# RWKV scan of a hybrid decoder: some 64x64 products moved to the other head's partitions, and the first transposed inverse made by TensorE

## What is computed

```
def step(S, inp):
    r_t, w_t, k_t, v_t, kk_t, a_t = inp
    sa = jnp.einsum('bhvk,bhk->bhv', S, -kk_t)
    S = (S * w_t[:, :, None, :] + sa[..., None] * (kk_t * a_t)[:, :, None, :]
         + v_t[..., None] * k_t[:, :, None, :])
    return S, jnp.einsum('bhvk,bhk->bhv', S, r_t)
...
S, y = lax.scan(step, S0.astype(jnp.float32), (tm(rh), tm(decay), tm(kh), tm(vh), tm(kk), tm(ah)))
```

## Time and profile before

| | us |
|---|---|
| median of three runs | 3128.39 (3128.33 to 3129.97) |
| the profiled execution | 3125.38 |
| its span, first to last instruction | 3123.7 |
| the scan's first score product and last state product | 920.6 and 1189.0 |
| from one step to the next | 16.4 |

### The profile page before, as it was taken

One profiled execution on the slowest core, in us unless ns is written; L12 is line 12 of the kernel. 1 busy time (PEld: TensorE's weight loads), 2 busy tenths in 40 slices (PEclk: granted clock), 3 DMA queues, 4 the chain that ended last, 5 costly groups with the idle time before them and its releaser, 6 DMA issues.

```text
span 3123.7 us, 75122 instructions
## 1 busy us (share of the span) xinstructions
PE 2958.1 (95%) x30609; PEld 2794.0 (89%) x30609; DVE 1578.3 (51%) x2270; ACT 1048.9 (34%) x2014; POOL 1336.7 (43%) x954
## 2 busy tenths in 40 slices
PE   6998999988989998899999899989999899899998
PEld 6997999978878886799998699879999799799998
DVE  3436666037258876576612251466660344476612
ACT  3224333225443333433322443343332322433322
POOL 3443544442335554254544263434444344254543
PEclk8999999999999999999999899999999899899999
DMA  7552333543420002333355232433336343133332
GB/s 260 166 166 86 89 95 100 189 117 113 145 49 4 4 4 65 108 96 95 88 181 150 69 123 78 139 116 92 92 100 202 111 151 108 55 96 94 90 88 88
DMA packets 465625, 332.69 MB, mean 107 GB/s; under 512 B 19914, under 2 KB 435608, under 8 KB 465122
## 3 DMA queue, kind: packets, MB, share of 16 engines
q1 hardware_dynamic: 461400, 325.24, 33.9%
q10 hardware_dynamic: 4010, 4.22, 0.6%
HBM read 319.62 MB, written 10.20 MB: 106 GB/s over the span
## 4 chain that ended last, share of the span: by engine, by line
PE 61%; DVE 5%; ACT 2%; issue 1%; POOL 0%; DVEq 0%; ACTq 0%
PE bank L1578 32%; PE bank L1586 16%; PE bank L2026 6%; PE bank L1601 1%; DVE h L2497 1%; PE bank L1539 1%; PE bank L1876 1%; PE bank L1607 1%; DVE proj L2442 0%; DVE mmt L2775 0%; PE bank L1668 0%; DVE rstd L2388 0%; DVE bd_B L2744 0%; PE bank L2167 0%; DVE bd_K L2739 0%
## 5 line engine op out<-in xcount | busy, mean ns | idle before, releaser
L741 POOL TENSOR_TENSOR w_lo<-w_raw,w_hi 128x1024 fp32r<-128x1024 f32 x404 | 1023.3, 2534 | 1199.4 <-ACT w_hi L937 1178.9
L1578 PE MATMUL bank<-u_hi,w_hi 128*128 128x260 f32 x4064 | 831.5, 286 | 15.7 <-ACT w_hi L937 9.4
L1578 PE MATMUL bank<-u_lo,w_hi 128*128 128x260 f32 x4064 | 821.9, 283 | 0.0
L1578 PEld LDWEIGHTS bank<-u_hi,w_hi 128*128 128x128 f32 x4064 | 623.4, 188 | 31.1 <-issue 19.3
L1578 PEld LDWEIGHTS bank<-u_lo,w_hi 128*128 128x128 f32 x4064 | 626.2, 188 | 1.8
L937 ACT ACTIVATE w_hi<-w_raw 128x1024 fp32r<-128x1024 f32 x402 | 424.4, 1056 | 477.6 <-PE bank L1586 240.7
L1586 PE MATMUL bank<-u_hi,w_lo 128*128 128x260 f32 x4064 | 528.1, 282 | 0.0
L1586 PEld LDWEIGHTS bank<-u_hi,w_lo 128*128 128x128 f32 x4064 | 502.4, 187 | 1.7
L1578 PE MATMUL bank<-hid_hi,w_hi 128*128 128x260 f32 x1664 | 337.6, 284 | 0.0
L1578 PE MATMUL bank<-hid_lo,w_hi 128*128 128x260 f32 x1664 | 335.0, 283 | 0.0
L2927 DVE TENSOR_TENSOR csb<-proj 128x520 f32 (+1 forms) x42 | 29.7, 707 | 486.6 <-ACT proj L1002 486.6
(11 more groups left out here) (461 smaller groups left out, 4062.9 us busy)
## 6 DMA issues: line engine op xcount, KB each, us to landing
w_raw<-in_ffn_w_up_dram SPq DMA_DIRECT2D x176, 512.0 KB, 3.6
...
```

What stands on the lines that cost most here:

```text
L741: pool.tensor_tensor(w_lo[:, s, :, :], w_raw[:, s, :, :], w_hi[:, s, :, :].bitcast(F32), ALU.subtract).then_inc(lo_done, 1)
L1578: pe.matmul(tile_ps[slot][half][0:width, 0:HALF], w_hi[:, s, k, 0:width], x[:, k0 + k, half * HALF:(half + 1) * HALF], start=start and k = ...
```

## The change

All of it is in the scan. A product that reads one head's partitions and writes the other's is called crossed.

- t1, the right side and the new transpose are crossed; so t1 and `rhs_sb` lie on the other head's partitions. t1 goes to columns 128 to 255 of bank 2g instead of 0 to 127.
- The transposed inverse is kept on the other head's partitions too.
- The first update product (to the inverse) reads the other head's partitions and writes its own: crossed, into bank 2g. The second (to the transpose) reads and writes the other head's: straight, into bank 2g+1. VectorE's addition reads both banks, which are now one tensor `banks`, with a four-dimensional pattern. u is crossed and comes back to its own partitions.
- GpSimd makes only the first inverse, with one multiplication by `low_mask` and one addition over all four tiles. TensorE transposes it behind the keys (`turn_inverse`, four tiles, crossed, into the upper half of bank 0). ScalarE copies it to `mmt` ahead of the y copy (`turned_inverse`). The counts of `tok_done` and `tok_ready` go up by one a step.
- New waits: TensorE's t1 and VectorE's addition at level 0 wait for that copy; TensorE waits for `inv_ready` already at the transpose, with y and the state update behind it.
- `inv_mask` and the ScalarE copies that filled it, once at the start, go.

The diff, without the declaration and the filling of `inv_mask`:

```diff
@@ -250,3 +249,4 @@
 
-        bank = [ctx.enter_context(nc.psum_tensor(f"bank{i}", [P, 512], F32)) for i in range(8)]
+        banks = ctx.enter_context(nc.psum_tensor("banks", [P, 8 * 512], F32))
+        bank = [banks[:, i * 512:(i + 1) * 512] for i in range(8)]
         tile_ps = [(bank[0], bank[1]), (bank[2], bank[3])]
@@ -849,11 +849,7 @@
                         idb = head_ident[:, :].unsqueeze(1).to_broadcast([P, 4, HD])
-                        both = inv_mask[:, :, :].rearrange("p two t -> p (two t)").unsqueeze(1).to_broadcast([P, 2, P])
-                        for g in range(2):
-                            gs = slice(2 * g, 2 * g + 2)
-                            pool.tensor_tensor(mmt[q][:, gs, :], sc[q][:, gs, 0:2 * HD], both, ALU.mult)\
-                                .then_inc(inv_masked, 1)
-                        for g in range(2):
-                            pool.wait_ge(inv_masked, 2 * w + g + 1)
-                            mv = mmt[q][:, 2 * g:2 * g + 2, :].rearrange("p i (two t) -> p (i two) t", two=2)
-                            pool.tensor_tensor(mv, mv, idb, ALU.add).then_inc(inv_ready, 1)
+                        pairs = low_mask[:, :].unsqueeze(1).to_broadcast([P, 4, HD])
+                        inv = mmt[q][:, :, 0:HD]
+                        pool.tensor_tensor(inv, sc[q][:, :, 0:HD], pairs, ALU.mult).then_inc(inv_masked, 1)
+                        pool.wait_ge(inv_masked, w + 1)
+                        pool.tensor_tensor(inv, inv, idb, ALU.add).then_inc(inv_ready, 1)
 
@@ -1347,3 +1341,3 @@
                         for i, (n, bk) in enumerate(((2, 4), (0, 1), (1, 3))):
-                            act.wait_ge(tok_done, 3 * w + i + 1)
+                            act.wait_ge(tok_done, 4 * w + i + 1)
                             act.activation(tok[:, :, n * HD:(n + 1) * HD],
@@ -1351,2 +1345,8 @@
 
+                    def turned_inverse(w, q):
+
+                        act.wait_ge(tok_done, 4 * w + 4)
+                        act.activation(mmt[q][:, :, HD:2 * HD], bank[0][:, 4 * HD:8 * HD].rearrange("p (i t) -> p i t", i=4),
+                                       ACT.Copy).then_inc(tok_ready, 1)
+
                     def scan_step(c, q, one_more, two_more):
@@ -1358,3 +1358,3 @@
                                 act.activation(t1[:, 2 * g:2 * g + 2, :],
-                                               bank[2 * g][:, 0:2 * HD].rearrange("p (i t) -> p i t", i=2),
+                                               bank[2 * g][:, 2 * HD:4 * HD].rearrange("p (i t) -> p i t", i=2),
                                                ACT.Copy).then_inc(t1_ready, 1)
@@ -1375,2 +1375,4 @@
                            .then_inc(uu_ready, 1)
+                        if one_more:
+                            turned_inverse(w + 1, 1 - q)
                         act.wait_ge(y_mm, w + 1)
@@ -1383,2 +1385,3 @@
 
+                    turned_inverse(0, 0)
                     tokens_out(0)
@@ -2022,2 +2025,6 @@
 
+                    def far(rs):
+
+                        return heads[1 - rs.start // HD]
+
                     def both(out, left, right, start=True, stop=True):
@@ -2054,2 +2061,10 @@
 
+                    def turn_inverse(w, q):
+
+                        pe.wait_ge(inv_ready, w + 1)
+                        for i in range(4):
+                            mm = both(lambda rs: bank[0][far(rs), (4 + i) * HD:(5 + i) * HD], lambda rs: mmt[q][rs, i, 0:HD],
+                                      lambda rs: ident[rs, rs])
+                        mm.then_inc(tok_done, 1)
+
                     def turn_values(c, q):
@@ -2070,7 +2085,8 @@
                                 else:
-                                    pe.wait_ge(inv_ready, 2 * w + g + 1)
+                                    pe.wait_ge(inv_ready, w + 1)
+                                    pe.wait_ge(tok_ready, 4 * w + 1)
                                 for i in range(2):
                                     z = 2 * g + i
-                                    mm = both(lambda rs: bank[2 * g][rs, i * HD:(i + 1) * HD], lambda rs: ct[rs, z, :],
-                                              lambda rs: mmt[q][rs, z, 0:HD])
+                                    mm = both(lambda rs: bank[2 * g][far(rs), (2 + i) * HD:(3 + i) * HD],
+                                              lambda rs: ct[rs, z, :], lambda rs: mmt[q][rs, z, 0:HD])
                                 mm.then_inc(t1_mm, 1)
@@ -2079,5 +2095,5 @@
                                 pe.wait_ge(st_updated, w + 1)
-                                pe.wait_ge(tok_ready, 3 * w + 1)
+                                pe.wait_ge(tok_ready, 4 * w + 2)
                                 for i in range(4):
-                                    o = lambda rs: bank[4][rs, i * HD:(i + 1) * HD]
+                                    o = lambda rs: bank[4][far(rs), i * HD:(i + 1) * HD]
                                     both(o, lambda rs: b["ZR"][rs, i, 0:HD], lambda rs: rw_ST[rs, 4 * q + i, :], True, False)
@@ -2086,3 +2102,3 @@
                                 mm.then_inc(rhs_mm, 1)
-                                pe.wait_ge(tok_ready, 3 * w + 3)
+                                pe.wait_ge(tok_ready, 4 * w + 4)
                             if one_more and lvl < 4:
@@ -2099,9 +2115,8 @@
                                 for i in range(2):
-                                    z = 2 * g + i
-                                    o = bank[2 * g + 1]
+                                    z, cs = 2 * g + i, slice(i * HD, (i + 1) * HD)
                                     if lvl < len(LEVELS) - 1:
-                                        both(lambda rs: o[rs, 2 * i * HD:(2 * i + 1) * HD], lambda rs: mmt[q][rs, z, HD:2 * HD],
-                                             lambda rs: t1[rs, z, :])
-                                    mm = both(lambda rs: o[rs, (2 * i + 1) * HD:(2 * i + 2) * HD], lambda rs: t1[rs, z, :],
-                                              lambda rs: mmt[q][rs, z, HD:2 * HD])
+                                        both(lambda rs: bank[2 * g][rs, cs], lambda rs: mmt[q][far(rs), z, HD:2 * HD],
+                                             lambda rs: t1[far(rs), z, :])
+                                    mm = both(lambda rs: bank[2 * g + 1][far(rs), cs], lambda rs: t1[far(rs), z, :],
+                                              lambda rs: mmt[q][far(rs), z, HD:2 * HD])
                                 mm.then_inc(d_mm, 1)
@@ -2116,4 +2131,4 @@
                                 pe.wait_ge(mmt_ready, 10 * w + 9 + i // 2)
-                            mm = both(lambda rs: bank[5][rs, i * HD:(i + 1) * HD], lambda rs: mmt[q][rs, i, HD:2 * HD],
-                                      lambda rs: rhs_sb[rs, i, :])
+                            mm = both(lambda rs: bank[5][rs, i * HD:(i + 1) * HD], lambda rs: mmt[q][far(rs), i, HD:2 * HD],
+                                      lambda rs: rhs_sb[far(rs), i, :])
                         mm.then_inc(u_mm, 1)
@@ -2122,2 +2137,3 @@
                             turn_keys(qn)
+                            turn_inverse(w + 1, qn)
                         pe.wait_ge(uu_ready, w + 1)
@@ -2144,2 +2160,3 @@
                     turn_keys(0)
+                    turn_inverse(0, 0)
                     pe.wait_ge(sample_columns_ready, 1)
@@ -2771,7 +2788,11 @@
                                 else:
-                                    dve.wait_ge(inv_ready, 2 * w + g + 1)
-                                dv = bank[2 * g + 1][:, 0:4 * HD].rearrange("p (i t) -> p i t", i=2)
-                                lo = 0 if lvl < len(LEVELS) - 1 else HD
-                                dve.tensor_tensor(mmt[q][:, gs, lo:2 * HD], mmt[q][:, gs, lo:2 * HD], dv[:, :, lo:2 * HD],
-                                                  ALU.add).then_inc(mmt_ready, 1)
+                                    dve.wait_ge(tok_ready, 4 * w + 1)
+                                if lvl < len(LEVELS) - 1:
+                                    dv = banks[:, 1024 * g:1024 * g + 1024].rearrange("p (b c) -> p b c", b=2)[:, :, 0:2 * HD]
+                                    dv = dv.rearrange("p b (i t) -> p i b t", i=2)
+                                    inv = mmt[q][:, gs, :].rearrange("p i (b t) -> p i b t", b=2)
+                                else:
+                                    dv = bank[2 * g + 1][:, 0:2 * HD].rearrange("p (i t) -> p i t", i=2)
+                                    inv = mmt[q][:, gs, HD:2 * HD]
+                                dve.tensor_tensor(inv, inv, dv, ALU.add).then_inc(mmt_ready, 1)
                             if one_more and lvl < 4:
@@ -2780,3 +2801,3 @@
                                 dve.wait_ge(exp_done, w + 3)
-                                dve.wait_ge(tok_done, 3 * w + 3)
+                                dve.wait_ge(tok_done, 4 * w + 3)
                                 build(c + 1, q)
```

3 lines of the change are left out of this document (removed).

## The result

The changed kernel takes 3107.61 us, the median of five runs from 3104.74 to 3112.66, against 3128.39 for the kernel before in the same comparison (five runs, 3123.04 to 3129.97): a ratio of 0.9935, with a 95% interval of 0.9923 to 0.9947. Predicted were 3108 and a range of 3102 to 3122. The number fits. What it was added up from does not: one term was far too small, another was missing, and the two nearly cancel. That the number came out is luck.

What follows compares the result with a forecast made beforehand. TensorE was taken to bound levels 0 and 1 and the tail, VectorE levels 2 and 3. Fourteen full steps at 1.20 (16.8), step 14 1.8, step 15 0.9, start 0.9: 3128.4 - 20.4 = 3108 us; range 3102 to 3122.

Steps and rivals of the forecast that it cites:

- Updates in four quarters, 8 slots to 4: Scan levels: a pair's update records take 4 slots (one record of each head together), gaining 0.23 us where TensorE bounds.
- Level 1, 0.35: Scan level 1: scores run beside t1, updates start 0.12 us earlier, and four quarters give 0.23; 0.35 a step.
- Level 0, 0.57: Scan level 0: scores run beside the right side, updates follow at once in 4 slots; 0.57 us a step.
- Levels 2 and 3, 0.01: Scan levels 2 and 3: VectorE runs without a gap for 4.96 us, so TensorE's gain is worth only 0.01.
- The added transpose, hidden: Scan tail: the transpose's 0.47 us on TensorE runs beside the keys, so nothing behind it waits.
- Tail, 0.27: Scan tail: crossed u need not wait for the values, so keys start earlier; 0.27 us after giving back 0.06.
- Step 14 and step 15: Last two scan steps: 1.8 us for the one without builds, 0.9 for the last, 0.23 in four levels.
- Start, 0.9: Start of the scan: GpSimd's masks and additions become half, less a transpose and a copy; 0.9 us gained.
- in order: Rival, whole scan: four quarters work but no product passes another; -0.3 us a step, 3122; chance 0.14.
- the quarters conflict: Rival, scan updates: crossed and straight products cannot run together, updates keep 8 slots, transpose adds; 3135; chance 0.06.
- VectorE gives it back: Rival within the forecast, scan: slower VectorE additions or lateness at level 0; 3108 to 3114; chance 0.66 with the forecast.
- the case where only neighbours pass: Partial case, scan: u is hidden but scores do not pass; 3113 to 3118; chance 0.10.

Runs made afterwards that it cites:

- the kernel with nothing crossed: The changed kernel with t1, right side, u, updates and turned inverse all kept on their own head's partitions; 3131.74 us against 3125.13 for the kernel before, ratio 1.0020.
- the kernel with VectorE first: The kernel before, with a one-element GpSimd product delaying GpSimd's products at levels 3 and 4 behind VectorE's builds; 3121.98 us against 3125.13, ratio 0.9988.

## Why the prediction was right, and where it was not

- **Updates in four quarters, 8 slots to 4.** Right, by the rows of level 1 above and, from the other side, by the kernel with nothing crossed.
- **Level 1, 0.35.** Measured 0.40.
- **Level 0, 0.57.** Measured 0.45. The step that failed is "they run beside the right side": the scores pass by some three slots and no more, so a part of them still stands between the right side and the updates (the last start of the right side at 1005.89, the first update at 1005.99). That is a half of what is lacking. The other half comes from every second step, in which the addition starts 0.10 later, 2.31 behind the state addition, though TensorE's updates stand where they stand in the others. VectorE's work ahead of it ends later there by as much (1020.95 - 1018.98 = 1.97, against 1006.22 - 1004.36 = 1.86), but it then sits idle 0.34 in both; what holds it is not shown.
- **Levels 2 and 3, 0.01.** The term that was mis-sized: 0.69. "VectorE is the bound for 4.96 us" read merged rows, two additions in 0.89 and two in 0.86, as one piece of work each. In them the second addition waited 0.13 and 0.10 for TensorE; the earlier trace rows had 0.74 for two at level 3, which would have said so. The rest, 0.22 for each of two builds, was not in the sum in any form: I had left GpSimd as "no term", because nothing waited for it by a semaphore. Its place against VectorE was worth 0.4 us a step.
- **The added transpose, hidden.** Nearly: keys end their starts at 1016.26, y begins at 1016.39, ahead of the last transposes, which start up to 1016.56. Without it the scan is 2 to 3 us shorter, a part of which is its 32 instructions.
- **Tail, 0.27.** Measured 0.15 in a step without a gap. The keys start 0.32 earlier relative to level 4, as worked out, and y 0.20 earlier; more is given back for the transpose than the 0.06 I had.
- **Step 14 and step 15.** 15.68 to 14.08, 1.6 for 1.8. In step 15 the distances gained 0.21, 0.19, 0.20 and nothing, not 0.23 four times: level 4 has one product a pair, so its four quarters were never to be had. Its end gained another 1.1, 4.12 from level 4 to st_end before and 3.04 after; but the kernel with VectorE first, which crosses nothing, has 3.02 and the one with nothing crossed 4.11, so that does not come from the crossing. VectorE's pieces meet GpSimd's long products there, and one of 512 elements took 1.83 us before and 0.79 after.
- **Start, 0.9.** Measured 0.57.
- **Not in the sum.** The supply of instructions, 0.5 us a step. The step was costed by its slots and waits, and not by its instructions; and no view that I read says how near a kernel is to the limit.

Fourteen full steps gained 17.3 us, predicted 16.8; with the first error alone put right the sum would have been some 9.5 us larger, with the second alone 7 smaller. The forecast's own terms gave 1.00 of the 1.68 us of an undisturbed step. The number held because what it had too small and what it left out were of one size, and that is luck. Two of the signs that it gave for being wrong or right say so too: the run from level 1 to level 3 was to stay at 4.9 and is 4.27, and y was to start at least 0.3 earlier relative to level 4 and starts 0.20 earlier.

Of the rivals, "in order" and "the quarters conflict" are excluded by the rows (transposes ahead of keys, sixteen records in 0.24 us). Of "VectorE gives it back", the slower additions did not come (0.42 as before); being late at level 0 may be behind the 0.10 of every second step, 0.7 us in all. Between forecast and in-order stood the case where only neighbours pass; the measured passing, three slots, is of that kind, but it was worth more than the case allowed, since scores pass as well as u. The granted clock is 1.00 in every stretch above, as before.

Open is what sets the time of a block. The packets take 0.9 to 1.4 us each and start 0.4 to 2.5 us after TensorE has passed the place. With the 1.2 to 1.6 from landing to the next instruction, that makes 2.5 to 5.5, but why the start varies, no run here tells.
